# Two of four softmax normalisations per attention unit moved from VectorE to Pool, in a fused two-block kernel on one core

## The reference, cut to what matters

```python
scores = jnp.where(valid, einsum(q, k) * D ** -0.5, -inf)      # local: 128 queries see 256 keys
probs  = softmax(concatenate([scores, sink]))[..., :-1]         # sink: one extra logit per head
o_swa  = einsum(probs, v)                                       # 8 heads, 2 key/value heads
p      = softmax(einsum(q, mem_k) * D ** -0.5)                  # memory: 4 heads, 256 keys
o_mem  = einsum(p, mem_v)
```

## Time and profile before

| | us |
|---|---|
| median of 3 runs | 3115.86 (3112.82 to 3118.89) |
| the profiled execution: span from first to last instruction | 3116.1 |
| local attention, 176.0 to 261.4 of the span | 85.4 |
| memory attention, 299.0 to 347.5 of the span | 48.5 |

### The profile page before, as it was taken

How to read it: one execution, slowest core, us unless ns; L and a number is a source line. 1 busy time by engine, 2 the same in 40 slices (tenths; PEclk the granted TensorE clock), 3 DMA queues, 4 the chain that set the end, 5 groups by cost and what they waited for, 6 DMA issues and landing times.

```text
span 3116.1 us, 36793 instructions
## 1 busy us (share of the span) xinstructions
PE 2836.1 (91%) x13150; PEld 2272.7 (73%) x13150; DVE 1455.1 (47%) x2871; ACT 932.0 (30%) x1906; POOL 263.3 (8%) x430
## 2 busy tenths in 40 slices
PE   4976879996999799999999989998898999999997
PEld 4745758883567678888888867777776888888886
DVE  5274569996433333233322353333843444433445
ACT  5154342222220132222222244223414222222222
POOL 0221411221004100000000000002200000000000
PEclk9988969997999899999999989999888999999999
DMA  4011022333634302011111112221040201110111
GB/s 156 19 31 50 28 62 76 103 101 113 221 116 154 124 20 81 28 54 54 54 37 43 54 44 89 69 74 49 15 169 11 77 28 54 54 54 27 54 40 61
DMA packets 119645, 213.99 MB, mean 69 GB/s; under 512 B 10852, under 2 KB 39100, under 8 KB 119284
## 3 DMA queue, kind: packets, MB, share of 16 engines
q1 hardware_dynamic: 107188, 185.30, 18.2%
q10 hardware_dynamic: 8064, 14.68, 1.3%
q0 software_dynamic: 4288, 12.64, 1.2%
HBM read 178.94 MB, written 33.64 MB: 68 GB/s over the span
## 4 chain that ended last, share of the span: by engine, by line
PE 70%; DVE 13%; issue 7%; ACT 5%; DMA 3%; POOL 2%; SPq 0%; DVEq 0%; ACTq 0%
PE bank L1594 20%; PE bank L1595 19%; PE bank L1596 19%; PE bank L1820 3%; DVE w_lo L980 1%; ACT w_hi L600 1%; PE bank L1807 1%; PE bank L1785 1%; DVE cmpj L1184 1%; DVE stage L1272 1%; DVE probs L1085 1%; DMA w_raw<-in_w_ff 1%; PE bank L1795 1%; DMA w_raw<-in_w_in 1%; DVE mx L1071 1%
## 5 line engine op out<-in xcount | busy, mean ns | idle before, releaser
L1594 PE MATMUL bank<-h_hi,w_hi 128*128 128x512 f32 (+1 forms) x1312 | 513.1, 391 | 18.5 <-DVE h_lo L1386 7.9
L1595 PE MATMUL bank<-h_lo,w_hi 128*128 128x512 f32 (+1 forms) x1312 | 510.6, 389 | 0.0
L1596 PE MATMUL bank<-h_hi,w_lo 128*128 128x512 f32 (+1 forms) x1312 | 510.3, 389 | 0.0
L600 ACT ACTIVATE w_hi<-w_raw 128x512 fp32r<-128x512 f32 (+3 forms) x440 | 255.0, 616 | 762.4 <-PE bank L1596 550.3
L1594 PE MATMUL bank<-w_hi,hid_hi 128*128 128x512 f32 x1024 | 400.2, 391 | 8.2 <-DVEq L1345 8.0
L1595 PE MATMUL bank<-w_lo,hid_hi 128*128 128x512 f32 x1024 | 398.5, 389 | 0.0
L1596 PE MATMUL bank<-w_hi,hid_lo 128*128 128x512 f32 x1024 | 398.4, 389 | 0.0
L980 DVE TENSOR_TENSOR w_lo<-w_raw,w_hi 128x512 fp32r<-128x512 f32 (+3 forms) x384 | 246.6, 679 | 205.8 <-ACT w_hi L600 199.1
L1318 DVE TENSOR_TENSOR hid_lo<-bank,hid_hi 128x512 fp32r<-128x512 f32 x128 | 88.5, 692 | 510.4 <-ACT hid_hi L805 510.4
L1594 PEld LDWEIGHTS bank<-h_hi,w_hi 128*128 128x128 f32 x1312 | 248.7, 190 | 73.7 <-DVE h_lo L1386 8.7
L1595 PEld LDWEIGHTS bank<-h_lo,w_hi 128*128 128x128 f32 x1312 | 248.7, 190 | 51.0 <-issue 0.7
(11 more groups left out here) (374 smaller groups left out, 4004.0 us busy)
## 6 DMA issues: line engine op xcount, KB each, us to landing
w_raw<-in_w_ff SPq DMA_DIRECT2D x128, 256.0 KB, 3.0
w_raw<-in_w_in SPq DMA_DIRECT2D x104, 256.0 KB, 3.0
ada<-in_w_ada SPq DMA_DIRECT2D x24, 1024.0 KB, 5.3
w_raw<-in_w_mlp_in SPq DMA_DIRECT2D x64, 256.0 KB, 3.0
w_raw<-in_w_mlp_out SPq DMA_DIRECT2D x64, 256.0 KB, 3.0
gates_scratch<-gstage ACTq DMA_DIRECT2D x48, 256.0 KB, 2.0
stage<-gates_scratch SPq DMA_DIRECT2D x16, 768.0 KB, 5.1
w_raw<-in_w_out SPq DMA_DIRECT2D x32, 256.0 KB, 3.6
```

What stands on the lines that cost most here:

```text
L600: A_(W[par][0][:, p, 0:n], raw[:, p % NRAW, 0:n], ACT.Copy).then_inc(w_hi, 1)
L1594: mm(out, lh, rh, start=(i == 0), stop=False)
L1595: mm(out, lh, rl, start=False, stop=False)
L1596: last = mm(out, ll, rh, start=False, stop=(i == n - 1))
```

## The change

On VectorE the loop over four heads becomes one over heads 0 and 1; between the reciprocal and these stands a `sem_inc(at_rc)`, and from unit 2 on the sum L1082 also waits for `at_p2` of unit u-2. Pool waits for `at_rc`, multiplies heads 2 and 3, and raises `at_p2`; its order is the multiplications of unit u, then the store of unit u-2. TensorE's transposes wait for `at_p` and `at_p2`. Nothing else differs.

```diff
+        at_rc, at_p2 = sem("at_rc"), sem("at_p2")
...
+            def att_norm(u):
+                kind, b, g = UNITS[u]
+                nk = P if kind == "swa" and b == 0 else 256
+                pool.wait_ge(at_rc, u + 1)
+                for i in range(2, 4):
+                    l = nc.gpsimd.tensor_scalar(pr[:, u % 3, i, 0:nk], pr[:, u % 3, i, 0:nk], rs[:, u % 2, i:i + 1], None,
+                                                ALU.mult)
+                l.then_inc(at_p2, 1)
+
+            def attend(u0, u1):
+                for u in range(u0, u1 + 2):
+                    if u < u1:
+                        att_norm(u)
+                    if u0 <= u - 2:
+                        store(u - 2)
...
-                    for u in range(NSWA + 8):
-                        store(u)
+                    attend(0, NSWA)
+                    attend(NSWA, NSWA + 8)
...
+                if u >= 2:
+                    dve.wait_ge(at_p2, u - 1)
                 link(tt(rs[:, u % 2, :], rs[:, u % 2, :], es[:, u % 2, :], ALU.add))
                 link(nc.vector.reciprocal(rs[:, u % 2, :], rs[:, u % 2, :]))
-                for i in range(4):
+                dve.sem_inc(at_rc, 1)
+                for i in range(2):
...
                 pe.wait_ge(at_p, u + 1)
+                pe.wait_ge(at_p2, u + 1)
```

## The result

The changed kernel takes 3145.0 us (median of 4 runs, 3144.36 to 3147.94); the kernel before takes 3116.61 us beside it. The ratio is 1.0093, with a 95% interval of 1.0082 to 1.0105: slower by 28.4 us. I had forecast slower, by 7 us, with a range up to 3136. The direction held; the size is four times the forecast and lies outside the range.

The account below looks back on a forecast made before the run. VectorE's work was taken to bound local attention, a latency loop memory attention. Longer steps, 2.0 + 1.1 + 2.7 = 5.8 us, plus 0.6 first use and 0.4 Pool beside VectorE, gave +6.8 on 3116.1: 3123 us, range 3115 to 3136.

Parts of the forecast that it names:

- What bounds it: Local attention: VectorE's work, 4.87 us a unit, with a 4.68 us loop close behind; memory attention: the loop, 5.15 us.
- VectorE's part: Two of four multiplications leave VectorE: 0.6 us less work a unit, 4.3 left; gain capped at 0.19 us a local step.
- The hand-overs: Reciprocal's end to Pool's start 0.13 us, Pool to TensorE 0.05; the wait on at_p2 costs nothing by itself.
- The price X: One Pool multiplication of 128x256: 0.79 us, between the select's slope (0.71) and TENSOR_TENSOR's (0.87); upper bound 1.19, floor 0.60.
- The sum: Attention steps lengthened: local 2.0 and 1.1 us, memory 2.7, plus small terms; +6.8 us on 3116.1, giving 3123.
- small terms: Added to the steps' 5.8 us: a first use of Pool's multiplication, 0.6 us, and Pool running beside VectorE, 0.4 us.
- the first use: Pool's first multiplications in the narrow first units cost extra, between 0 and 1.5 us, taken as 0.6.
- Pool beside VectorE: Slowing beside VectorE's multiplications: 0.01 us for each of 42 instructions in full-width steps, 0.4 us in all.
- rival 4: TensorE falls to its lower clock ahead of attention transposes: about 1.3 us a step, 3136 to 3150 us; chance 0.06.
- rival 3: VectorE's and Pool's multiplications exclude each other: Pool starts 0.43 us later, 21 steps, +9 us, 3132; chance 0.07.
- Rival 1: Not slower: Pool's multiplication price nearly all fixed cost, local decision point 0.70 us; 3114 to 3119 us; chance 0.30.

Follow-up runs that it names:

- e6: Changed kernel with VectorE's normalisation of unit u-1 put ahead of attn_lo of unit u-3: 3114.6 us, ratio 0.9988 to the kernel before.
- e7: Kernel before, all four multiplications on VectorE, with normalisation of unit u-1 put ahead of attn_lo of unit u-3: 3107.2 us, ratio 0.9967.
- e1: Changed kernel with eight unread identity products on TensorE ahead of each unit's transposes, filling its idle: 3126.6 us.
- e2: Kernel before with eight unread identity products on TensorE ahead of each unit's transposes: 3112.6 us.
- e5: Changed kernel with VectorE's own two multiplications left out, Pool's two kept: 3148.9 us in one run.
- e4: Changed kernel with one head multiplied on Pool and three on VectorE: 3119.7 us, ratio 1.0012 to the kernel before.
- e9: e6 with filling products on TensorE ahead of the transposes, four in a local unit, two in a memory unit: 3098.8 us.
- e10: e7 with filling products on TensorE ahead of the transposes, four in a local unit, two in a memory unit: 3100.1 us.
- e11: Kernel before with two extra multiplications by 1.0 on VectorE ahead of its four, lengthening TensorE's idle without Pool arithmetic: 3150.2 us.
- e12: e11 with eight filling products on TensorE ahead of each unit's transposes: 3129.0 us.
- e8: Changed kernel with one head on Pool, three on VectorE, and normalisation of unit u-1 ahead of attn_lo of unit u-3: 3111.4 us.
- e3: Changed kernel with Pool's two multiplications left out, Pool only passing the semaphore on: 3105.6 us, ratio 0.9960 to the kernel before.

## Why the prediction was wrong

**What bounds it.** Right. VectorE's own work and a second loop only 0.19 us shorter, closed by `attn_lo` ahead of the reciprocal; e6 and e7 show that it is that order.

**VectorE's part.** 0.6 us fewer forecast, 0.54 measured (1.21 to 0.67), and 0.11 us go to the `sem_inc`, which I had put down as sequencer work without a price. It did not matter, since VectorE was no longer the bound.

**The hand-overs.** 0.31 us from the reciprocal's start to Pool's was 0.34 (212.98 to 213.32). Pool to TensorE, 0.05, was 0.10 (213.32 + 1.95 = 215.27, to 215.37). The new wait on `at_p2` cost nothing, as forecast: Pool's pair ends at 215.27, and the next sum on VectorE, which waits for the pair before that one, comes at 219.67.

**The price X.** The first of the two steps that failed: mis-sized. I took 0.79 us, the middle between two slopes; it is 0.89 alone and 0.95 beside VectorE, so 2X is 1.95 with its end, not 1.58. The better neighbour was the one I had moved away from: the slope of Pool's `TENSOR_TENSOR` gave 0.87. From 0.595 us at 129 columns to 0.89 at 256 are 2.3 ns a column, steeper still. The reason that I gave for a flatter slope, one tensor read instead of two, did not hold. An estimate from the best case in the Trainium skill, GPSIMD Engine Reference, section 3.1, was 1.5 ns a column; the trace does not agree, with its 2.3.

**The sum.** The form was right: local loop = 3.11 us + the way to the transposes = 5.50, measured 5.48 at full clock. With the way at 2.40 us instead of 1.94 the latency is 14 us (e1 against e2), where the sum has 6.8 with its small terms. The error of the sum's own terms is therefore 7 us, or 9 if e2's longer steps are allowed for. Of the small terms, the first use (0.6) did not show: Pool's first pair took 1.24 us and its second 1.26. Pool beside VectorE was put at 0.01 us an instruction and was 0.06 (e5).

**The clock.** This is the step that failed most. Measured are 28.4 us and forecast 6.8; of the 21.6 us between, 13.5 are the clock's (18.4 that the change gained by the fillers, less the 4.9 that the kernel before gained by them); the 1 us that is left is within the noise. The sum puts the clock at nothing. It stood there as rival 4, with its price a step right (1.3 us forecast, 6.87 - 5.48 = 1.39 measured), and transposes of 1.9 us in the steady part were named as a sign of being wrong, which came; but it had a chance of 0.06 and was left out of the range, because I let it begin at an idle of 2.6 us. I took that from the steps that showed a slow transpose in the kernel before (idles of 2.55 and 2.75 us, one of them) and looked at nothing shorter, for the trace had nothing between 1.7 and 2.55 in the full-width units. Even that boundary was not in the trace: one memory unit after an idle of 2.55 us had transposes of 1.09 us (at 336.19), and one local unit after an idle of 0.91 us had transposes of 1.97 (at 194.90), the unit behind an idle of 2.56. An idle between 1.7 and 2.55 was unknown ground, and the range should have held it: at my own X the idle was 2.0.

**The lock, rival 3.** Neither as cheap as I took it nor as dear as the rule has it. The pairs add 0.13 and 0.14 us to each other. The Trainium skill, SBUF — State Buffer, section Who interferes with whom, has the engine that issues second wait for the whole instruction of the other, where VectorE's is in a 2-port mode. If VectorE's multiplications are in such a mode, which no run here shows, the trace does not agree: Pool's first starts 0.01 us after VectorE's first (213.32 and 213.31), and VectorE's second does not wait out Pool's 0.89 us. In e4 the same effect, over three multiplications, was 0.34 us and cost the experiment its gain.

**Rival 1, not slower.** Its point of decision, X = 0.70, was far off; the argument for it, that Pool hardly held VectorE up in the recurrence, says nothing on Pool's price.

## What to carry to other kernels

Before moving work from a bound engine to a slower one beside it, look for the loop that passes through that work, and price it in latency and not in busy time: here VectorE lost 0.5 us of work a unit and the unit became 0.6 us longer. If an order on one engine closes the loop, exchange that first; exchanging two steps was worth 10 us with no work moved (e7). With it in place moving the work cost 7 us while TensorE's idle was left as it was (e6 against e7), and was worth nothing that could be told once the idle was filled (e9 against e10). And whatever lengthens TensorE's regular wait can cost its clock: price that as a step of its own, and try filling the wait, which was worth 4.9 us even to the kernel before.

## What the runs showed of the hardware

- TensorE's clock in a loop of some 5 us: idle 1.7 us a step, it held in nearly every step (kernel before, e4); idle 2.25 to 2.34, it fell to the lower level in most steps (the change, e11), so that the transposes took 1.94 us instead of 1.06; idle 0.35 to 0.45, it held in every filled steady step (e1, e12). The idle just ahead does not decide it alone: at 2.34 us it also held (235.94), and after 0.91 us it had also fallen (kernel before, 194.90). 2.05 us of useless products a step gave back 18 to 21 us.
- Pool's multiplication by a scalar per partition: 0.6 us at 128 and 129 columns, 0.89 at 256 (e5).
- Pool's and VectorE's multiplications side by side slow each other by 0.13 to 0.14 us a pair; of VectorE's the first is not slowed (0.26 or 0.27 us to the next), the second takes 0.41 and a third 0.46 (the change, e4, e8). Pool's store alone stretched VectorE's four from 1.06 to 1.21 us (e7, where it comes later, against the kernel before).
- A `sem_inc` of VectorE's between two dependent instructions costs it 0.11 us (e3 against the kernel before).
